# Finding slots by matmuls and adding experts' rows by accumulating gathers

## What is computed

```
scores = sigmoid(h @ router_w)                 # 16 experts in 4 groups, one group chosen
expert = top 2 of the group; gate = scores[expert] / sum
order = argsort(expert); tok = order // 2; xs = h[tok]
y = (silu(xs @ w_gate[e]) * (xs @ w_up[e])) @ w_down[e]
y = y * gate[order]
x = x + mod_gate * zeros.at[tok].add(y)        # mod_gate: one row for latent, one for context tokens
```

## Time and profile before

| What | us |
|---|---|
| Median of 3 runs (4219.74 to 4226.65) | 4221.15 |
| The profiled execution's own time | 4226.27 |
| Its span in the profile | 4224.5 |
| TensorE busy (share of the span) | 3820.8 (90%) |
| VectorE busy | 1195.1 (28%) |
| ACT busy | 778.5 (18%) |
| GpSimd busy | 498.1 (12%) |

### The profile page before, as it was taken

The page is one execution under the profiler, slowest core; times in us unless marked ns, Lnnn a source line. Parts: engine busy times, 40 slices in busy tenths (PEclk is TensorE's granted clock), DMA queues, the critical chain, the costliest instruction groups (busy, mean ns, idle before and its releaser), DMA issues. The chain is left out here.

```text
span 4224.5 us, 54615 instructions
## 1 busy us (share of the span) xinstructions
PE 3820.8 (90%) x22812; PEld 2931.6 (69%) x22812; DVE 1195.1 (28%) x3091; ACT 778.5 (18%) x1692; POOL 498.1 (12%) x497
## 2 busy tenths in 40 slices
PE   6999999995799999999569999999794999999994
PEld 3666767643667999988446666666543899997873
DVE  3333333413110011111255555555513111111114
ACT  2222333300000000000113333333300000000001
POOL 3001000033200000000240111011033000000003
PEclk8999999996899999999879999999896999999997
DMA  5459100204434567789520000000104555679994
GB/s 166 167 215 344 56 23 20 71 25 146 158 127 146 183 210 253 261 283 311 188 68 11 16 16 16 16 16 6 46 31 147 186 183 188 211 260 310 311 310 161
DMA packets 450586, 618.95 MB, mean 147 GB/s; under 512 B 27480, under 2 KB 346472, under 8 KB 444080
## 3 DMA queue, kind: packets, MB, share of 16 engines
q1 hardware_dynamic: 420360, 514.33, 37.1%
q0 software_dynamic: 22240, 73.58, 4.8%
q10 hardware_dynamic: 7752, 27.59, 1.8%
HBM read 548.45 MB, written 67.39 MB: 146 GB/s over the span
## 5 line engine op out<-in xcount | busy, mean ns | idle before, releaser
L1687 PE MATMUL ps<-item_xT,expert_ring 128*128 128x128 f32 (+9 forms) x8192 | 1170.3, 306 | 1.1 <-DVE item_xT L1764 1.1
L1687 PEld LDWEIGHTS ps<-item_xT,expert_ring 128*128 128x128 f32 x8192 | 1116.4, 192 | 57.2 <-issue 5.7
L1720 PE MATMUL ps<-item_aT,expert_ring 128*128 128x144 f32 (+8 forms) x2304 | 407.7, 332 | 0.0
L1771 DVE TENSOR_TENSOR item_aT<-item_silu,ps 128x128 f32<-128x128 f32 (+9 forms) x256 | 83.7, 327 | 1070.1 <-ACT item_silu L1741 1070.1
L1720 PEld LDWEIGHTS ps<-item_aT,expert_ring 128*128 128x128 f32 x2304 | 359.1, 193 | 24.4 <-issue 0.8
L1741 ACT ACTIVATE item_silu<-ps 128x128 f32<-128x128 f32 (+9 forms) x256 | 78.9, 308 | 1315.3 <-PE ps L1687 1315.3
L386 PE MATMUL ps<-hT,oT 128*128 128x512 f32 x576 | 254.6, 602 | 1.4 <-PEq L994 0.7
L744 PE MATMUL ps<-hT,w_group 128*128 128x512 f32 (+1 forms) x704 | 254.7, 515 | 0.4 <-PEq L304 0.4
L1086 PE MATMUL ps<-hT,w_group 128*128 128x512 f32 (+1 forms) x576 | 234.6, 551 | 0.4 <-PEq L304 0.4
L1637 POOL DMA_INDIRECT gathered<-h_rows,slot_idx x55 | 52.4, 953 | 1525.4 <-PE ps L1670 1514.9
L1782 DVE COPY item_y<-ps 128x512 f32<-128x512 f32 (+3 forms) x106 | 69.0, 684 | 572.4 <-PE ps L1700 395.6
(11 more groups left out here) (210 smaller groups left out, 4011.7 us busy)
## 6 DMA issues: line engine op xcount, KB each, us to landing
expert_ring<-in_expert_w_gate SPq DMA_DIRECT2D x128, 1024.0 KB, 5.2
expert_ring<-in_expert_w_up SPq DMA_DIRECT2D x128, 1024.0 KB, 8.0
expert_ring<-in_expert_w_down SPq DMA_DIRECT2D x64, 2048.0 KB, 7.8
oT<-in_mod_w SPq DMA_DIRECT2D x40, 1024.0 KB, 6.5
slot_out<-rows POOLq DMA_DIRECT2D x7, 4096.0 KB, 49.1
w_group<-in_w_qkv SPq DMA_DIRECT2D x48, 512.0 KB, 3.8
slot_out<-item_y ACTq DMA_DIRECT2D x35, 512.0 KB, 7.6
h_rows<-hr SPq DMA_DIRECT2D x18, 512.0 KB, 2.6
```

The lines of the kernel that those rows point to most:

```text
L1687: m = nc.tensor.matmul(gub(j, b, w), ring[:, b // 2, k, w * 256 + (b % 2) * P:w * 256 + (b % 2 + 1) * P], xT[:, k, 0:C], start=k == 0, sto ...
L1720: m = nc.tensor.matmul(yb(j, d), ring[:, 4 + d // 4, f, (d % 4) * P:(d % 4 + 1) * P], aT[:, f, 0:C], start=f == 0, stop=f == FB - 1)
L1771: nc.vector.tensor_tensor(aT[:, b, 0:C], sg[:, b % 2, 0:C], gub(j, b, 1), ALU.mult).then_inc(s_a, 1)
```

## The change

The rooms begin at multiples of 128 slots, so that a slot is a block and a row in it. Routing no longer scatters. VectorE writes marks: for each (token, choice) a row of 128 that is 1 at the slot's row, and a row of 65 (layer 1: 56) that at the slot's block holds the token's number, and another that holds its gate. TensorE multiplies the one by the other over all tiles, and out come three tables with a row for each place in a block and a column for each block: token, gate if it is a latent token, gate if it is a context token. VectorE copies them from the banks. The first item's gathers are issued in the routing block. The gates are worked out earlier, before the wait for the counts.

In the experts the index is a column of the token table, without a read from DRAM. VectorE's copy of each half of the output becomes a product with the slot's gate and the mods' row; in layer 0 there are two such products (latent and context) and a sum. In the norms with combining GpSimd gathers from `ys` straight onto `x_res`, adding; the second gather of a tile waits until the first has landed. ACT takes both halves of the transposed tile, and VectorE and GpSimd each add the shift to one half. L433, L464, L466 and L468 go. The clearing of the lists in the first block goes as well; `ys`, which is cleared during layer 0's attention, becomes 8320 rows long in place of 7424.

```diff
-SLOT0 = tuple([sum(r[:n]) for n in range(NE)] for r in ROOMS)
+BLOCKS0 = tuple([sum(-(-m // P) for m in r[:n]) for n in range(NE)] for r in ROOMS)
+SLOT0 = tuple([n * P for n in b] for b in BLOCKS0)
 RESTS = tuple(2 * TILES[l] * P // REST + NE for l in range(2))
 SLOTS = tuple(SLOT0[l][FIXED] + (RESTS[l] + 1) * REST for l in range(2))
+NBLOCKS = tuple(n // P for n in SLOTS)
...
-                        total = SLOTS[l] * 16
...
-                    y = sb(c, "y_pair", [P, 3, 2, D])
-                    gate = sb(c, "gate_rows", [P, 2, D])
-                    s_gr, s_m, s_c = (sem(c, n) for n in ("gate_rows_in", "y_first", "y_sum"))
+                    s_both = [sem(c, f"y_both{n}") for n in range(3)]
...
-                        if source == "combine" and at(u, 0):
-                            act.wait_ge(s_in[u % 3], 32 * (u // 3 + 1))
-                            nc.scalar.activation(y[:, u % 3, 0, :], y[:, u % 3, 0, :], ACT.Copy, scale=gates[:, u, 0:1]).then_inc(s_m, 1)
...
+                            elif source == "combine":
+                                act.wait_ge(s_both[t % 3], 16 * (t // 3 + 1))
...
+                            if source == "combine":
+                                act.wait_ge(s_tr, 2 * t + 2)
+                                nc.scalar.activation(hT[:, 4:8, col(t)], bank(tbank(t) + 1).rearrange("p (k n) -> p k n", n=P),
+                                                     ACT.Copy).then_inc(s_evd, 1)
...
-                            y0, y1 = y[:, u % 3, 0, :], y[:, u % 3, 1, :]
-                            dve.wait_ge(s_m, u + 1)
-                            nc.vector.scalar_tensor_tensor(out=y0, in0=y1, scalar=gates[:, u, 1:2], in1=y0, op0=ALU.mult, op1=ALU.add).then_inc(s_c, 1)
-                            dve.wait_ge(s_c, u + 1)
-                            nc.vector.tensor_tensor(y0, y0, gate[:, 1 if u >= LT else 0, :], ALU.mult).then_inc(s_g, 1)
-                            dve.wait_ge(s_g, u + 1)
-                            nc.vector.tensor_tensor(x[:, u, :], x[:, u, :], y0, ALU.add).then_inc(s_x, 1)
...
-                            if source is None:
+                            if mode == "mix":
...
-                        if mode != "final" and at(u, L_EV):
+                        if mode != "final" and source != "combine" and at(u, L_EV):
...
-                    def gather(t):
-                        if t >= 3:
-                            pool.wait_ge(s_x, t - 2)
-                        for i in range(2):
-                            nc.gpsimd.indirect_dma_start(out=y[:, t % 3, i, :], out_offset=None, in_=ys,
-                                                         in_offset=bass.IndirectOffsetOnAxis(slots[:, t, i:i + 1], 0)).then_inc(s_in[t % 3], 16)
+                    def add(t, i):
+                        if i:
+                            pool.wait_ge(s_in[t % 3], 16 * (t // 3) + 16)
+                        nc.gpsimd.indirect_dma_start(out=x[:, t, :], out_offset=None, in_=ys, compute_op=ALU.add,
+                                                     in_offset=bass.IndirectOffsetOnAxis(slots[:, t, i:i + 1], 0)).then_inc((s_both if i else s_in)[t % 3], 16)
                     if source == "combine":
-                        gather(0)
-                        gather(1)
+                        for t in range(3):
+                            add(t, 0)
                     for u in step_range:
-                        if source == "combine" and u + 2 < T:
-                            gather(u + 2)
+                        if source == "combine" and u < T:
+                            add(u, 1)
+                            if u + 3 < T:
+                                add(u + 3, 0)
...
-                            pool.wait_ge(s_sc, 2 * t + 2 if source is None else t + 1)
-                            w = HALF if source is None else D
+                            pool.wait_ge(s_sc, 2 * t + 2 if mode == "mix" else t + 1)
+                            w = HALF if mode == "mix" else D
...
+                    for v in range(2 - l):
+                        sp.dma_start(rows[:, v, :], mods[l, v, 5 * D:6 * D].partition_broadcast(P)).then_inc(s_tok, 16)
...
+                    for i, oh in enumerate((oh1, oh2)):
+                        ch.then(v.tensor_tensor(t16[:, :], sc[:, :], oh[:, :], ALU.mult))
+                        ch.then(v.tensor_reduce(gt[:, i * T:(i + 1) * T], TE(t16), AX.X, ALU.add))
+                    ch.then(v.tensor_tensor(t1[:, :], gt[:, 0:T], gt[:, T:2 * T], ALU.add))
+                    ch.then(v.reciprocal(t1[:, :], t1[:, :]))
+                    for i in range(2):
+                        ch.then(v.tensor_tensor(gt[:, i * T:(i + 1) * T], gt[:, i * T:(i + 1) * T], t1[:, :], ALU.mult))
...
+                    dve.wait_ge(s_tok, 16 * (3 - l))
+                    ch.then(v.tensor_scalar(blk[:, :, :], slots[:, 0:T, :].rearrange("p t i -> p i t"), 7, None, ALU.logical_shift_right))
+                    ch.then(v.tensor_copy(blkf[:, :, :], blk[:, :, :]))
+                    ch.then(v.scalar_tensor_tensor(out=row[:, :, :], in0=blkf[:, :, :], scalar=-128.0, in1=both(slotf), op0=ALU.mult, op1=ALU.add))
+                    n2 = lambda z: z.rearrange("p i t -> p (i t)").unsqueeze(2)
+                    blks = con[:, C_IOTA:C_IOTA + NB] if NB <= 64 else tok[:, NT:NT + NB]
+                    marks = at_blk[:, :, :, :].rearrange("p n w b -> p w n b")
+                    for i in range(2):
+                        ch.then(v.tensor_tensor(at_row[:, i * T:(i + 1) * T, :], bc(n2(row[:, i:i + 1, :]), [P, T, P]),
+                                                bc(tok[:, NT:NT + P].unsqueeze(1), [P, T, P]), ALU.is_equal))
+                        n = slice(i * T, (i + 1) * T)
+                        gated, named = marks[:, 0, n, :], marks[:, 1, n, :]
+                        ch.then(v.tensor_tensor(gated, bc(n2(blkf[:, i:i + 1, :]), [P, T, NB]), bc(blks.unsqueeze(1), [P, T, NB]), ALU.is_equal))
+                        ch.then(v.tensor_tensor(named, gated, bc(tok[:, 0:T].unsqueeze(2), [P, T, NB]), ALU.mult))
+                        ch.then(v.tensor_tensor(gated, gated, bc(gt[:, n].unsqueeze(2), [P, T, NB]), ALU.mult))
+                        CH_BLK[i] = ch.n
+                    dve.wait_ge(s_inv, 1)
+                    v.tensor_copy(token[:, :], TOK).then_inc(s_idx, 1)
+                    ch.then(v.tensor_copy(gate[:, 0, :], GX))
+                    if l == 0:
+                        ch.then(v.tensor_copy(gate[:, 1, :], GC))
...
+                    for n in range(2 * T):
+                        if n % T == 0:
+                            pe.wait_ge(s_ch, CH_BLK[n // T])
+                        if n % T < LT:
+                            m = nc.tensor.matmul(bank(5, 0, 2 * NB), at_row[:, n, :], at_blk[:, n, :, :].rearrange("p w b -> p (w b)"),
+                                                 start=n == 0, stop=n == 2 * T - 1)
+                        else:
+                            nc.tensor.matmul(bank(4, 0, NB), at_row[:, n, :], at_blk[:, n, 0, :], start=n == LT, stop=n == 2 * T - 1)
+                            m = nc.tensor.matmul(bank(5, NB, 2 * NB), at_row[:, n, :], at_blk[:, n, 1, :], start=False, stop=n == 2 * T - 1)
+                    m.then_inc(s_inv, 1)
...
-                    pool.wait_ge(s_tok, 16)
-                    pool.wait_ge(s_ch, CH_SLOT[0])
-                    for t in range(T):
-                        for i in range(2):
-                            nc.gpsimd.indirect_dma_start(out=idx_dram[l], out_offset=bass.IndirectOffsetOnAxis(slots[:, t, i:i + 1], 0),
-                                                         in_=tok[:, t, :], in_offset=None).then_inc(s_slot, 16)
-                    pool.wait_ge(s_slot, 16 * 2 * T)
+                    pool.wait_ge(s_idx, 1)
+                    for n in range(-(-ROOMS[l][0] // P)):
+                        r1 = min(P, ROOMS[l][0] - n * P)
+                        nc.gpsimd.indirect_dma_start(out=xg[0:r1, n, :], out_offset=None, in_=h_dram,
+                                                     in_offset=bass.IndirectOffsetOnAxis(token[0:r1, n:n + 1], 0)).then_inc(s_xg, 16)
...
-                    for n, (r0, r1) in enumerate(blocks(j)):
-                        pool.dma_start(idx[0:r1 - r0, n, :], idx_dram[l][bass.ds(slot(j) + r0, r1 - r0), :]).then_inc(s_ix, 16)
-                    pool.wait_ge(s_ix, moved(j + 1))
...
+                    if isinstance(j, int):
+                        index = token[:, first_block(j):first_block(j) + len(blocks(j))]
+                    else:
+                        nc.gpsimd.tensor_copy(idx[:, :], token[:, bass.ds(first_block(j), 1)]).then_inc(s_ix, 1)
+                        pool.wait_ge(s_ix, j - FIXED)
+                        index = idx
...
+                    def gated(j, h, b, r0, r1, gates):
+                        src = bank(4 + h if by_rows(j) else rowb[b])[0:r1 - r0, :]
+                        cols = slice(h * HALF, (h + 1) * HALF)
```

(24 more changed lines are left out.)

88 lines of the change are left out of this document (39 added, 49 removed).

## The result

The changed kernel takes 4212.9 us (median of 11 runs, 4209.3 to 4219.6), the kernel before 4224.8 (11 runs, 4219.7 to 4227.8). The medians lie 11.9 us apart. The ratio is 0.9976, 95% interval 0.9966 to 0.9985, and follows the means, which lie 10.2 us apart. The forecast was 18.5 us less and 4203. The profiled executions have spans of 4211.1 and 4224.5, 13.4 apart.

A forecast was written before the change was run, and what follows sets the result against it. TensorE, busy 90% of the span, was taken as the bound. The terms -2 - 19 - 17 + 24 + 1.5 - 13 + 7 gave -18.5 us: 4203 against the median of 4221.15, range 4182 to 4232.

The forecast's parts named there:

- Start, -2: In the first block: no longer clearing the two lists brings the last weight piece earlier, 0 to 2.1 us, taken as -2.
- routing, -19 and -17: From last cast of slots to first transpose: inverting by matmuls instead of scatters saves 19 us in layer 0, 17 in layer 1.
- the rival in which it costs what it saves: Routing: matmuls wait on marks, or the block end waits for the table; no change to 4212, no separate chance given.
- The stall, "+24 in 11 of 16 items": Layer 0's experts: three-instruction copies delay the fifth transposition back, 1.25 to 2.5 us an item, +24 us in all.
- TensorE has no slack there, so it counts in full: Layer 0's experts: the waits of TensorE were added to the time at their own length, +24 us.
- the upper bound of +29: Layer 0's experts: the largest stall allowed, +29 us, if hand-overs cost more than put.
- The rival without a stall: Layer 0's experts: VectorE's three instructions fit and TensorE doesn't wait; -43 us, 4178, chance 0.05.
- An adding gather costs two reads, 2.6 us: Both combining norms: an accumulating gather reads the row and the tile, 2.6 us against 1.3 for a plain one.
- both its rivals: Combining norms: a gather costs what a plain one does (4184, chance 0.2), or three passes, 3.9 us (4245, slow gathers 0.15).
- Norm after layer 0's experts, -13: First combining norm: a tile every 6.0 us instead of 7.5, ending at 2172 where it was 2185.3, -13 us.
- From there TensorE needs 38 us: Norm after layer 0's experts: TensorE's time from tile 5's arrival, put at 2134, to the end at 2172.
- Last norm, +7: Final combining norm: adding gathers and stores fill the queues, 51 us + 2.5 until the last add; +7 us.

## Why the prediction went as it did

Direction and range were right; the size was short, 18.5 us forecast and 11.9 measured (between medians of 11 runs each). The forecast of 4203 stood on a median of 3 runs, 4221.15, which 11 runs put at 4224.8. On that it would have been 4206, so the sum itself misses by about 7 us and not by 10. That it misses by no more is luck in part: the stall cost 12.6 us more than its terms, and the first of the norms and the mixer gave back most of that for reasons that the forecast doesn't have.

- *Start, -2; routing, -19 and -17.* Right: -2.8, -19.1 and -17.2 (second profile: -19.1 and -16.0). Nothing in inverting was late: the rival in which it costs what it saves is out. (The gates have four short instructions and not five; with four they add up to the 2.3 us put.)
- *The stall, "+24 in 11 of 16 items".* The waits themselves are exact: 11, 23.7 us. **The step that failed is the next one, "TensorE has no slack there, so it counts in full".** A wait of TensorE there counts for more than itself. It brought 12.5 us of slower matmuls at a lower granted clock (0.57 in the 4 us behind the wait shown), and the upper bound of +29 allowed only for hand-overs. The row that could have warned is in the earlier trace rows: TensorE idle, granted clock 0.50. The rival without a stall is out.
- *An adding gather costs two reads, 2.6 us.* Right in kind, 2.86 measured, and both its rivals are out: not a plain gather's cost (1.48 to 1.54), and not three passes.
- *Norm after layer 0's experts, -13.* Measured -17.4 with the first square as worked out, and a step of 6.2 us where 6.0 was put. Tile 5 comes 57.8 us after the first gather, as good as forecast (58.4); what was overdone is the end, "From there TensorE needs 38 us": it took 34.7 to the next stage. The 38 us were taken from a trace in which part of them ran at the low clock, behind the wait of 3.52 us for tile 9. With that wait down to 0.45 us the last 32 passes took 13.90 us where they had taken 15.92. The passes in the changed kernel:

```profile
2170.20 13.90 PE L276 MATMUL ps<-hT,w_group 128*128 128x512 f32 x32
```

  The stretch from tile 9 to the end of the norm in the kernel before, at a granted clock of 0.84 (columns as in the earlier trace rows):

```profile
2167.60:2185.50 17.90, 17.67 (x40) 8.38 (x40) 0.69 (x1) 0.60 (x1) 0.00 (x0) 0.84 0.00 0
```

  The same in the changed kernel, at 1.00:

```profile
2169.30:2184.40 15.10, 14.80 (x40) 6.79 (x40) 0.00 (x0) 1.44 (x4) 0.04 (x1) 1.00 0.00 1
```

  So the same mechanism cost time in the experts and gave some back here. The step's length is near the forecast, but not for its reason alone: in the whole stage GpSimd waited 5.7 us for landings and 7.1 for the squares behind them. Its issue, put at 1.25 us a gather, took 1.86 in the mean, so that GpSimd was at work for 5.7 of the 6.2 us of a step.
- *Last norm, +7.* Measured +10.6 and +8.5 in two profiles. It took 2.6 us of queue time for a gather where 2.86 were needed, and 16 gathers make 4 us of that. Its bound from below was wrong: a norm with plain gathers was put at -3.4, and the run without adding shows -10.1.
- *The mixer of layer 1* shows -6.1 without a change in its code. Two profiles of before against ten give -3.6. Most of it lies in one place: after a wait of TensorE of about 4 us, some 468 us into the stage, the clock stood at half for 10 us in both profiles of before and for 7 us or less in all ten others, and the matmuls of the next 90 us or so took 93.2 and 93.4 us against 89.3 to 90.7. So it is not the execution alone; what the change left behind for that place is open.

With the stall's term at 38.1 the sum is -5.9. The norm's -4.4 beyond the forecast, the last norm's +3.6, the mixer's -6.1 and -0.6 of small terms make it the -13.4 of the two profiles.

## What to carry to other kernels

Where TensorE never waits, price a new wait by its length and by the matmuls behind it: here 23.7 us of waits cost 36, because the granted clock fell as well, and filling them with matmuls that nobody reads was 9 us faster than standing still. Before adding instructions between a result and the release of its bank, look for the part of them that doesn't need the result, and do it ahead. An adding gather is not a free addition: it halves the queues' rate and lengthens its issue on GpSimd, so it can pay only where the adding engine is the limit and the queues aren't, and no run here shows such a place: in the norm after layer 0's experts two additions on VectorE were level with it (91.8 against 92.5 us), and in the last norm they were better by 17.4 us.

## What the runs showed of the hardware

- Behind six of eleven waits of TensorE, all six of 2.2 to 2.4 us, in a stretch that had run at 2.4 GHz, the granted clock fell to half, 0.57 on average over the next 4 us in the item shown. Behind the other five, of 1.2 to 2.2 us, it didn't. By room, the down matmuls (busy us, mean ns) went from 69.1 to 76.6 us in four items of 144 columns, but stayed at 27.1 in the one of 240, whose wait was 1.18 us.

```profile
L1739 PE MATMUL ps<-item_aT,expert_ring 128*128 128x144 f32 x512 | 76.6, 310 | 0.0
...
L1739 PE MATMUL ps<-item_aT,expert_ring 128*128 128x240 f32 x128 | 27.1, 366 | 0.0
```

- An indirect gather that adds takes GpSimd 1.54 us to issue where a plain one takes 0.94, and lands in 8.6 to 10.3 us where that takes 5.4 to 6.9 (medians by stage). Its bytes held the DMA engines for 2.86 us against 1.48 to 1.54.
- VectorE's and GpSimd's instructions hold each other up: a scaling of 1024 elements took 1.28 us alone and up to 2.29 beside GpSimd's add, and GpSimd's issue of an adding gather 2.40 beside that scaling.
